# Windowed attention in a hybrid RWKV-7 layer: 128-query blocks with TensorE turns, or 32-query groups over 160 keys with VectorE turns

## The chip, the cores and the metric

The kernel runs on one core of one Trainium2 chip. The metric is the device time of one execution in microseconds (us); lower is better. A profile of one execution gives the start and length of each instruction on TensorE (PE for its matmuls, PEld for its weight loads), VectorE (DVE), ScalarE (ACT) and the transfers that SyncE (SP) issues.

## What is computed

One layer over 2048 tokens of width 1024: an RMS norm, one input projection of 2560 columns, an RWKV-7 recurrence of 8 heads beside windowed attention of 8 query heads on 2 key heads (64 wide each), an output projection, an MLP of width 4096, a gated embedding and a last norm. Of the attention, this is what the change touches:

```python
qi = jnp.arange(BLOCK)[:, None] + BLOCK        # BLOCK = WINDOW = 128
ki = jnp.arange(2 * BLOCK)[None, :]
dist = qi - ki
valid = (dist >= 0) & (dist < WINDOW) & (blk * BLOCK + ki[None] - BLOCK >= 0)
logits = jnp.einsum('bnqhgd,bnkhd->bnhgqk', qb, kw) * ATTN_SCALE + bias
logits = jnp.where(valid[None, :, None, None], logits, -jnp.inf)
m = jnp.maximum(jnp.max(logits, axis=-1, keepdims=True), sink)
e = jnp.exp(logits - m)
probs = e / (jnp.sum(e, axis=-1, keepdims=True) + jnp.exp(sink - m))
out = jnp.einsum('bnhgqk,bnkhd->bnqhgd', probs, vw)
```

A query sees the 128 keys up to itself. A block of 128 queries therefore needs 256 keys; a group of 32 queries needs 160 (its own 32 and the 128 ahead of them, rounded to blocks of 32).

## The kernel before

**Two streams in one.** The 2048 tokens are 16 tiles of 128. The projection (`proj`, four blocks of 512 tokens) and everything behind the mixing (`fin`, four blocks) are long rows of large matmuls of 512 columns, each product computed three times from a split into a high and a low part. One weight chunk is 24 such matmuls; ACT makes its high part (line 991), DVE its low part (line 1312). The mixing of a tile (`mix`, recurrence and attention) is many small operations with long chains between engines. `side_by_side` interleaves them by hand: every engine's program yields after each half chunk of the large work ("a piece", 12 large matmuls) and after each of 27 steps of a tile, and the lists BESIDE_PROJ and BESIDE_FIN say after how many pieces of the large work each step of a tile comes. BESIDE_PROJ places tiles 0 to 3 beside the rest of the projection; BESIDE_FIN places four tiles beside each of the first three `fin` blocks (called here the first to fourth tile of a block). Two steps with the same number have no large matmuls between them. All engines follow the same list, each in its strict order; `Marks` are counting semaphores with one name for each finished operation. The last `fin` block has no tiles beside it.

**The steps around attention, on TensorE.** Step 9: `av` (697), `keys` (the tile's values turned by one 128x128 transpose, 702), `att0` (scores of two of four query-head pairs, line 605: 64-row tiles, 256 keys). Steps 10 to 14: `mz0` to `mz4` (713), five levels of a triangular inverse, 32 matmuls in 32x32 tiles each, in the four diagonal places of the array. With `mz2` goes `turn0` (614, eight 128x128 transposes of probabilities), with `mz3` go `pv0` (622, probabilities by values) and `att1` (605). Step 15: `q` (728). Step 16: `b` (735) and `turn1`. Step 17: `pv1`, `uw` (748 and 754). Steps 18 to 21: `sa0` (762), `grow0` (770, 771), `sa1`, `grow1`, then `y_in` and `y`.

**On VectorE.** Each level is three dependent operations: z (1507), up (1510) and m (1514, a transpose in 32x32 blocks); `mz` of level l waits for m of level l. `logits(n)` (1388 to 1403) comes in steps 9 and 13, `probabilities(n)` (1407 to 1411) in steps 11 and 15, the copy `wT` (1552) between `uw` and `sa0`, the copy `sa` (1415) between `sa0` and `grow0`. The DVE's share of the large work (w_lo 1312; 1634 and 1637 in the first MLP matmul; 1622 where the norm is applied) stands between the steps.

**On ScalarE.** exps (1078, 1080), the copies of the turned probabilities (`pt`), of the result (`att`) and of the values (`vk`), all at line 1084.

Of the kernel before, what the change touches and what calls it, by code (L numbers as in the profile page):

```python
# [9 lines left out]
ALU = mybir.AluOpType  # L10
# [24 lines left out]
LEVELS = 5  # L35

# [68 lines left out]
class Marks:  # L105
# [12 lines left out]
    def done(self, n, step):  # L118
# [14 lines left out]
MIX_PE = (["lora", "gate", "norm", "spread", "bonus", "beta", "alpha", "kappa"] + upto("score", 4) + ["av", "keys", "att0", "mz0", "mz1",  # L133
           "mz2", "turn0", "mz3", "pv0", "att1", "mz4", "q", "b", "turn1", "pv1", "uw",
           "sa0", "grow0", "sa1", "grow1", "y_in", "y", "out"])
MIX_ACT = ["tanh", "sig_g", "kk_sq", "sw", "av", "nrm", "kk_wide", "p_inc", "p_inv", "p_exc", "gate", "beta_t", "avt", "vk",
           "exp0", "esink0", "pt0", "att0", "exp1", "esink1", "pt1", "att1", "y_rms"]
# [3 lines left out]
MIX_DVE = (["kk_raw", "cum", "ascale", "kk_max", "kk_inv", "cumx", "kmod", "v_t", "kk", "kka", "alpha", "beta", "rk", "kappa", "ends", "rho", "yb", "alpha_t", "kappa_t"]  # L141
           + upto("mask", 4) + ["init", "up0", "m0"] + logits_of(0) + level_of(1) + level_of(2) + probs_of(0) + level_of(3)
           + level_of(4) + logits_of(1) + [f"z{LEVELS}", "inv_t", "inv", "xt64", "q"] + probs_of(1)
           + ["b", "wT", "sa0", "grow0", "state0", "sa1", "grow1", "state1", "y_sum", "y_mean", "y", "y_sq", "y_var", "y_inv", "y_norm", "rw", "rw_yb", "rw_gate"])
MIX_STEPS = 27
# [16 lines left out]
for _turned, _last in (("turn0", "out1_3"), ("xt0", "ple1_3")):  # L162
# [18 lines left out]
BESIDE_PROJ = (3, 5, 5, 5, 6, 7, 9, 11, 13, 14, 15, 17, 19, 20, 22, 24, 26, 27, 27, 28, 29, 29, 29, 29, 29, 31, 31, 31, 34, 34, 34, 35,  # L181
# [3 lines left out]
BESIDE_FIN = (0, 1, 2, 4, 4, 4, 6, 6, 10, 12, 13, 16, 18, 22, 23, 25, 28, 29, 31, 32, 33, 34, 34, 35, 38, 38, 40, 40, 40, 44, 46, 46,  # L185
# [3 lines left out]


# [1589 lines left out]
```

## Time and profile before

| | |
|---|---|
| median of 3 runs | 2844.11 us (2841.38 to 2848.77) |
| profiled execution, span | 2842.6 us |
| TensorE matmuls busy | 2784.0 us, 98% |
| VectorE busy | 1737.4 us, 61% |
| ScalarE busy | 1167.5 us, 41% |
| mean DMA rate | 112 GB/s |

How to read it: matmuls overlap, and each is recorded for as long as it takes to come out of the array, so the cost of a group of them is the distance from its first start to the start of what follows, not the sum of their lengths. A float32 matmul that isn't a transpose leaves two records (a count of x8 is four matmuls). Merged rows of the timeline give start, length, engine, line, operands and count, and in square brackets how long the engine sat idle before it and who released it.

### The profile page before, as it was taken

Reading aid. Unit: us, or ns where it says so; the run is one execution under the profiler, and the core shown is the slowest. Engines: PE = TensorE matmul, PEld = TensorE weight load, DVE = VectorE, ACT = ScalarE, POOL = GpSimd, SP = SyncE. Lnnn points to the kernel's source line nnn. Section 1 sums busy time; section 2 is a strip of 40 time slices with the busy share of each in tenths; the row PEclk is TensorE's granted clock in tenths of the full one; section 3 lists DMA queues with packets and bytes.
Section 4 is the critical chain, followed back from the end, with each engine's and each line's share of the span. In section 5 each row is a group of like instructions: output and inputs, shape, how many; then the busy total and the mean of one; then the engine's idle time right before and its main releaser. Section 6 shows DMA issues by size and latency. Waiting matters only on the chain.

```text
span 2842.6 us, 54416 instructions
## 1 busy us (share of the span) xinstructions
PE 2784.0 (98%) x23651; PEld 2251.3 (79%) x23651; DVE 1737.4 (61%) x2886; ACT 1167.5 (41%) x1942; POOL 0.2 (0%) x4
## 2 busy tenths in 40 slices
PE   8999999999999999999999999999999999999998
PEld 6877777777878787878887777878887788888876
DVE  5476676756666565675756566766575655443335
ACT  4354344344433342564333334543343335332225
POOL 0000000000000000000000000000000000000000
PEclk9999999999999999999999999999999999999999
DMA  6553443453333232343332333423333225233332
GB/s 211 162 167 97 146 130 97 136 178 98 89 95 95 86 96 93 122 157 91 92 93 85 96 96 130 155 75 92 101 95 87 84 96 185 89 96 97 97 101 77
DMA packets 369738, 317.47 MB, mean 112 GB/s; under 512 B 47291, under 2 KB 322012, under 8 KB 369500
## 3 DMA queue, kind: packets, MB, share of 16 engines
q1 hardware_dynamic: 365104, 309.58, 35.7%
q10 hardware_dynamic: 4396, 4.41, 0.5%
q8 instruction: 187, 3.06, 0.4%
q14 instruction: 51, 0.42, 0.0%
HBM read 276.18 MB, written 39.32 MB: 111 GB/s over the span
## 4 chain that ended last, share of the span: by engine, by line
PE 78%; DVE 2%; DMA 1%; ACT 1%; issue 0%; SPq 0%; ACTq 0%
PE ps L829 13%; PE ps L833 12%; PE ps L832 12%; PE ps L871 9%; PE ps L875 8%; PE ps L874 8%; PE ps L713 1%; PE ps L583 1%; PE ps L586 1%; PE ps L587 1%; PE ps L605 1%; DMA wraw_f<-in_w_gate 1%; PE ps L614 1%; PE ps L622 1%; PE ps L685 1%; PE ps L628 1%
## 5 line engine op out<-in xcount | busy, mean ns | idle before, releaser
L1312 DVE TENSOR_TENSOR w_lo<-wraw_f,w_hi 128x1024 fp32r<-128x1024 f32 x408 | 498.8, 1222 | 405.4 <-ACT w_hi L991 404.5
L991 ACT ACTIVATE w_hi<-wraw_f 128x1024 fp32r<-128x1024 f32 x408 | 430.9, 1056 | 553.4 <-PE ps L829 462.8
L829 PE MATMUL ps<-w_hi,h_hi 128*128 128x512 f32 x1280 | 513.0, 401 | 7.2 <-DVE rw L1583 4.4
L833 PE MATMUL ps<-w_hi,h_lo 128*128 128x512 f32 x1280 | 499.6, 390 | 0.0
L832 PE MATMUL ps<-w_lo,h_hi 128*128 128x512 f32 x1280 | 498.8, 390 | 0.0
L871 PE MATMUL ps<-act_hi,w_hi 128*128 128x512 f32 x1024 | 408.4, 399 | 0.4
L875 PE MATMUL ps<-act_hi,w_lo 128*128 128x512 f32 x1024 | 399.3, 390 | 0.0
L874 PE MATMUL ps<-act_lo,w_hi 128*128 128x512 f32 x1024 | 398.9, 390 | 0.0
L829 PEld LDWEIGHTS ps<-w_hi,h_hi 128*128 128x128 f32 x1280 | 240.3, 188 | 62.8 <-issue 7.9
L833 PEld LDWEIGHTS ps<-w_hi,h_lo 128*128 128x128 f32 x1280 | 240.2, 188 | 52.3
L832 PEld LDWEIGHTS ps<-w_lo,h_hi 128*128 128x128 f32 x1280 | 240.7, 188 | 46.4
L1192 ACT ACTIVATE h_hi<-tmp 128x512 fp32r<-128x512 f32 x128 | 80.9, 632 | 405.7 <-DVE tmp L1634 405.7
L871 PEld LDWEIGHTS ps<-act_hi,w_hi 128*128 128x128 f32 x1024 | 192.2, 188 | 43.5 <-issue 3.7
L875 PEld LDWEIGHTS ps<-act_hi,w_lo 128*128 128x128 f32 x1024 | 192.2, 188 | 41.2
L874 PEld LDWEIGHTS ps<-act_lo,w_hi 128*128 128x128 f32 x1024 | 192.4, 188 | 37.5
L1637 DVE TENSOR_TENSOR h_lo<-tmp,h_hi 128x512 fp32r<-128x512 f32 x128 | 88.7, 693 | 159.5 <-ACT tmp L1193 159.5
L1634 DVE SCALAR_TENSOR_TENSOR tmp<-ps,stage_f 128x512 f32<-128x512 f32 x128 | 88.2, 689 | 117.5 <-PE ps L875 114.8
L583 PE MATMUL ps<-act_hi,w_hi 128*128 128x512 f32 x320 | 129.9, 406 | 5.5 <-DVE rw L1583 2.9
L583 PE MATMUL ps<-h_hi,w_hi 128*128 128x512 f32 x320 | 129.2, 404 | 2.8 <-DVE rw L1583 1.5
L829 PE MATMUL ps<-w_hi,act_hi 128*128 128x512 f32 x320 | 127.4, 398 | 2.7 <-DVE w_lo L1312 2.3
L587 PE MATMUL ps<-act_hi,w_lo 128*128 128x512 f32 x320 | 125.8, 393 | 0.0
L586 PE MATMUL ps<-act_lo,w_hi 128*128 128x512 f32 x320 | 125.8, 393 | 0.0
(231 smaller groups left out, 4078.8 us busy)
## 6 DMA issues: line engine op xcount, KB each, us to landing
wraw_f<-in_w_ff_up SPq DMA_DIRECT2D x256, 256.0 KB, 3.3
wraw_f<-in_w_ff_down SPq DMA_DIRECT2D x128, 512.0 KB, 4.0
wraw_f<-in_w_in SPq DMA_DIRECT2D x80, 512.0 KB, 4.3
zT<-tmp SPq DMA_DIRECT2D x80, 256.0 KB, 2.1
wraw_f<-in_w_out SPq DMA_DIRECT2D x32, 512.0 KB, 4.0
wraw_f<-in_w_gate SPq DMA_DIRECT2D x32, 512.0 KB, 5.1
zs<-zT SPq DMA_DIRECT2D x16, 896.0 KB, 6.6
h_lo<-mixT SPq DMA_DIRECT2D x4, 2048.0 KB, 8.1
```

The lines of the kernel that those rows point to most:

```text
L583: mm = T.matmul(dst, wh, hi[:, k, :], start=(k == 0), stop=False)
L586: T.matmul(dst, wh, lo[:, k, :], start=False, stop=False)
L587: mm = T.matmul(dst, wl, hi[:, k, :], start=False, stop=(k == DK - 1))
L829: mm = T.matmul(ps[:, j, :], ah, wh, start=(first and k == 0), stop=False)
L832: T.matmul(ps[:, j, :], ah, wl, start=False, stop=False)
L833: mm = T.matmul(ps[:, j, :], al, wh, start=False, stop=(final and k == 1))
L871: mm = T.matmul(ps[:, bank, :], wh, act_hi[:, k, :], start=(k == 0), stop=False)
L874: T.matmul(ps[:, bank, :], wh, act_lo[:, k, :], start=False, stop=False)
L875: mm = T.matmul(ps[:, bank, :], wl, act_hi[:, k, :], start=False, stop=(k == DK - 1))
L991: S.activation(w_hi[:, n % 2, :], raw[:, n % 4, :], ACT.Copy).then_inc(w_hi_done, 1)
L1312: V.tensor_tensor(w_lo[:, n % 2, :], raw[:, n % 4, :], w_hi[:, n % 2, :].bitcast(F32), ALU.subtract).then_inc(w_lo_done, 1)
L1637: V.tensor_tensor(h_lo[:, i, :], tmp[:, i % 2, :], h_hi[:, i, :].bitcast(F32), ALU.subtract).then_inc(fin_dve.mark(f"h_lo{g}_{i}"), 1)
```

## The change

- Scores: for each of four query-head pairs, each group of 32 queries is multiplied with its own 160 keys, for both key heads: 16 matmuls for each round, in tiles of 64 rows by 32 columns of the array, 160 columns moved. Before: 4 matmuls for each round, 64x128, 256 columns.
- The bias, the logits, the exps and the normalisation go over 160 instead of 256 keys.
- The probabilities are turned in 32x32 blocks by VectorE (`pt0`, `pt1`, two transposes of 128x640) instead of 16 TensorE transposes and two ACT copies. Values come by four transfers for each tile into `v_raw`, staggered by 32 keys for each 32 partitions, and one VectorE transpose of 128x640 (`v_turn`, step 10) makes `v_win`, in place of the TensorE turn and the ACT copy `vk`.
- Probabilities by values is one step of its own for both rounds (`pv`, step 17 of now 28): 40 matmuls in tiles of 32 rows by 64 columns, 128 columns moved, into four banks. It waits for `b` and `pt1`. One ACT copy (`att`) in place of two.
- `att1` moves from `mz3` to `mz1`; `logits(1)` moves from VectorE's step 13 (behind m4) to step 12 (behind m3, ahead of z4). `uw` and what follows moves one step down. The lists of places get 28 numbers for each tile.

```diff
-MIX_PE = ([...] + ["av", "keys", "att0", "mz0", "mz1",
-           "mz2", "turn0", "mz3", "pv0", "att1", "mz4", "q", "b", "turn1", "pv1", "uw",
+MIX_PE = ([...] + ["av", "att0", "mz0", "mz1", "att1",
+           "mz2", "mz3", "mz4", "q", "b", "pv", "uw",
-probs_of = lambda n: [f"{s}{n}" for s in ("den", "inv", "probs")]
+probs_of = lambda n: [f"{s}{n}" for s in ("den", "inv", "probs", "pt")]
...
                     def scores(r):
                         for j in (2 * r, 2 * r + 1):
-                            for kv in range(2):
-                                rows = half64(kv)
-                                mm = T.matmul(ps[:, M1 + kv, (j % 2) * 2 * P:(j % 2 + 1) * 2 * P], qT[rows, j, :], kvT[rows, 0, :],
-                                              start=True, stop=True)
+                            for i in range(P // SUB):
+                                for kv in range(2):
+                                    rows = half64(kv)
+                                    mm = T.matmul(ps[sub32(i), M1 + kv, (j % 2) * KEYS:(j % 2 + 1) * KEYS], qT[rows, j, sub32(i)],
+                                                  kT[rows, i * SUB:i * SUB + KEYS], start=True, stop=True)
...
+                    def probs_by_values():
+                        for m in range(SEEN):
+                            for i in range(P // SUB):
+                                for kv in range(2):
+                                    mm = T.matmul(ps[half64(kv), M0 + i, 0:P], v_win[sub32(i), m, half64(kv)],
+                                                  pt[sub32(i), kv, :, m * SUB:(m + 1) * SUB], start=(m == 0), stop=(m == SEEN - 1))
+                        mm.then_inc(mix_pe.mark("pv"), 1)
...
-                        if l == 2:
-                            turn_probs(0)
-                        if l == 3:
-                            probs_by_values(0)
+                        if l == 1:
+                            after(mix_dve, "logit0")
                             scores(1)
...
                     mm.then_inc(mix_pe.mark("b"), 1)
-                    turn_probs(1)
-                    yield
-
-                    after(mix_act, "att0")
-                    probs_by_values(1)
+                    yield
+
+                    after(mix_dve, "b")
+                    after(mix_dve, "pt1")
+                    probs_by_values()
+                    yield
+
                     after(mix_dve, "xt64")
-                    after(mix_dve, "b")
+                    after(mix_act, "att")
... (SyncE)
-                    sp.dma_start(kvT[:, :, at:], zT[RWT + PAIRS:ZT, :, t * P + at:(t + 2) * P].rearrange(
-                        "f p t -> p f t")).then_inc(qkv_in, 16)
+                    sp.dma_start(kT[:, at:], zT[RWT + PAIRS, :, t * P + at:(t + 2) * P]).then_inc(qkv_in, 16)
+                    if t:
+                        sp.wait_ge(*mix_dve.done(t - 1, "v_turn"))
+                    for i in range(P // SUB):
+                        m0 = 0 if t else P // SUB - i
+                        cols = slice(t * P + (i + m0) * SUB, t * P + (i + SEEN) * SUB)
+                        sp.dma_start(v_raw[sub32(i), :, m0 * SUB:], zT[ZT - 1, :, cols].rearrange("(b d) t -> d b t", d=SUB)).then_inc(qkv_in, 16)
... (VectorE)
+                        own(f"probs{n}")
+                        V.transpose(pt[:, :, 2 * n:2 * n + 2, :]..., logit...).then_inc(mix_dve.mark(f"pt{n}"), 1)
...
+                        if step == 10:
+                            dve.wait_ge(qkv_in, 16 * (2 + P // SUB) * (t + 1))
+                            V.transpose(v_win[...], v_raw[...]).then_inc(mix_dve.mark("v_turn"), 1)
                         if step == 11:
                             probabilities(0)
-                        if step == 13:
+                        if step == 12:
+                            own("pt0")
                             logits(1)
```

Of the new places these pairs have no large matmuls between them: `mz3` and `mz4` in the second and third tile of a block (59, 59 and 97, 97, as before); `uw` and `sa0` in the same tiles (66, 66 and 104, 104; before 65, 66 and 103, 104), since `pv` has `uw`'s old place; in tile 0 `uw`, `sa0`, `grow0` (28), in tile 1 all from `uw` to `y` (56), in tile 2 `uw` to `y` (85), in tile 3 `uw` and `sa0` (113). In tile 2 `mz2` and `mz3` have none either (79, as before).

## Rows read from the trace of the kernel before

**Rows 1.** The page: busy time by engine, and the chain that ended last.
```profile
PE 2784.0 (98%) x23651; PEld 2251.3 (79%) x23651; DVE 1737.4 (61%) x2886; ACT 1167.5 (41%) x1942; POOL 0.2 (0%) x4
...
PE 78%; DVE 2%; DMA 1%; ACT 1%; issue 0%; SPq 0%; ACTq 0%
```
**Rows 2.** Timeline of TensorE (start, length, line, operands): attention's operations in two tiles.
```profile
912.78 0.33 PE L702 MATMUL ps<-con,kvT 128*128 128x128 f32 x1
913.04 1.14 PE L605 MATMUL ps<-kvT,qT 64*128 64x256 f32 x8
914.10 0.50 PE L871 MATMUL ps<-act_hi,w_hi 128*128 128x512 f32 x1
...
1096.69 1.08 PE L622 MATMUL ps<-work,vk 128*64 128x256 f32 x8
1097.70 1.13 PE L605 MATMUL ps<-kvT,qT 64*128 64x256 f32 x8
...
1117.74 1.09 PE L614 MATMUL ps<-con,work 128*128 128x128 f32 x8
1118.59 0.47 PE L829 MATMUL ps<-w_hi,h_hi 128*128 128x512 f32 x1
```
**Rows 3.** Timeline of TensorE: groups in small tiles of the array.
```profile
1001.31 0.69 PE L802 MATMUL ps<-state,pp 64*64 64x64 f32 x32
...
1061.89 1.98 PE L685 MATMUL ps<-pp,work 64*64 64x128 f32 x64
...
1087.91 0.75 PE L713 MATMUL ps<-work,small 32*32 32x32 f32 x64
...
1091.55 0.75 PE L713 MATMUL ps<-work,small 32*32 32x32 f32 x64
```
**Rows 4.** VectorE's transpose of 128x512, by form (count, busy, mean ns).
```profile
L1456 DVE STREAM_TRANSPOSE v_t<-kappa_t 128x512 f32<-128x512 f32 x16 | 11.3, 705 | 0.0
```
**Rows 5.** SyncE's own waits: weight loads (us in total, times, longest).
```profile
SPq L374 <- DVE w_lo L1312: 1125.5, 236, 11.7
```
**Rows 6.** Timeline, TensorE and VectorE, levels 3 and 4 of a block's second tile.
```profile
818.20 0.45 DVE L1514 STREAM_TRANSPOSE small<-work 128x256 f32<-128x256 f32 x1
818.56 1.20 DVE L1312 TENSOR_TENSOR w_lo<-wraw_f,w_hi 128x1024 fp32r<-128x1024 f32 x1
819.11 0.75 PE L713 MATMUL ps<-work,small 32*32 32x32 f32 x64
...
821.88 0.75 PE L713 MATMUL ps<-work,small 32*32 32x32 f32 x64
821.99 1.29 DVE L1388 SCALAR_TENSOR_TENSOR work<-ps,bias 128x512 f32<-128x512 f32 x2 [0.72 <-PE ps L605]
...
824.92 0.42 DVE L1523 TENSOR_TENSOR work<-ps,work 128x256 f32<-128x256 f32 x1
```
**Rows 7.** The same levels in the block's third tile.
```profile
953.25 0.75 PE L713 MATMUL ps<-work,small 32*32 32x32 f32 x64
...
955.56 0.45 DVE L1514 STREAM_TRANSPOSE small<-work 128x256 f32<-128x256 f32 x1
956.06 0.75 PE L713 MATMUL ps<-work,small 32*32 32x32 f32 x64
```
**Rows 8.** Timeline, first tile of a block, where the MLP's norm is applied.
```profile
678.33 1.09 PE L614 MATMUL ps<-con,work 128*128 128x128 f32 x8 [0.76 <-DVE work L1411]
...
682.15 1.40 DVE L1622 SCALAR_TENSOR_TENSOR act_lo<-ps,par,act_hi 128x512 fp32r<-128x512 f32 x2
```
**Rows 9.** Timeline of TensorE, tile 2: `uw` with `sa0` right behind it.
```profile
450.45 1.15 PE L754 MATMUL ps<-work 64*64 64x64 f32 x32
...
452.39 0.68 PE L762 MATMUL ps<-state,work 64*64 64x64 f32 x16 [0.79 <-DVE work L1552]
```
**Rows 10.** A long wait of TensorE, and the window behind it (the column ahead of the last two: granted clock).
```profile
252.78 0.80 PE L583 MATMUL ps<-act_hi,w_hi 128*128 128x512 f32 x1 [2.90 <-DVE rw L1583]
...
252.00:256.00 4.00, 3.22 (x8) 2.57 (x9) 2.71 (x6) 0.96 (x3) 0.00 (x0) 0.50 0.66 192
```

More of the change, by code:

```diff
@@ L35 @@
 LEVELS = 5
+SEEN = P // SUB + 1
+KEYS = SEEN * SUB
 PV = {}
@@ L448, in mix @@
                             load_rw(t + 1)
-                        if step == 18:
-                            sp.wait_ge(*mix_act.done(t, "att1"))
+                        if step == 19:
+                            sp.wait_ge(*mix_act.done(t, "att"))
                             sp.dma_start(mixT[PAIRS:, :, t * P:(t + 1) * P].rearrange("f p t -> p f t"), attT).then_inc(att_stored, 16)
-                        if step == 22 and t < TILES - 1:
+                        if step == 23 and t < TILES - 1:
                             sp.wait_ge(*mix_pe.done(t, "grow1"))
                             load_v(t + 1)
-                        if step == 26:
+                        if step == 27:
                             sp.wait_ge(*mix_dve.done(t, "rw_gate"))
@@ L618, in probs_by_values @@
-                    def probs_by_values(r):
-                        after(mix_act, f"pt{r}")
-                        for b in range(2):
-                            for kv in range(2):
-                                mm = T.matmul(pv_ps[half64(kv), :], vk[:, (t + 1 + b) % 2, kv * HD:(kv + 1) * HD],
-                                              pt[:, kv, b, :, :], start=(b == 0), stop=(b == 1))
-                        mm.then_inc(mix_pe.mark(f"pv{r}"), 1)
+                            for i in range(P // SUB):
[3 more added lines that the diff above has]
+                                                  kT[rows, i * SUB:i * SUB + KEYS], start=True, stop=True)
@@ L699, in mix @@
                     mm.then_inc(mix_pe.mark("av"), 1)
-                    pe.wait_ge(qkv_in, 32 * (t + 1))
-                    for b in range(1 if t else 0, 2):
-                        mm = T.transpose(pv_ps[:, b * P:(b + 1) * P], kvT[:, 1, b * P:(b + 1) * P], ident)
-                    mm.then_inc(mix_pe.mark("keys"), 1)
+                    pe.wait_ge(qkv_in, 16 * (2 + P // SUB) * (t + 1))
                     scores(0)
@@ L749, in mix @@
                                      xt64[tok64(c), quad(f, a), :], start=True, stop=True)
-                    after(mix_act, "att1")
                     for h in range(HEADS):
@@ L1391, in logits @@
                             o.then_inc(set_up, 1)
-                            dve.wait_ge(set_up, 7 + n)
-                            o = V.tensor_scalar(logit[:, :, 0:P], logit[:, :, 0:P], NEG, None, ALU.add)
+                            dve.wait_ge(set_up, 8 + n)
+                            for i in range(P // SUB):
+                                before = logit[sub32(i), :, 0:P - i * SUB]
+                                o = V.tensor_scalar(before, before, NEG, None, ALU.add)
                         o.then_inc(mix_dve.mark(f"logit{n}"), 1)
@@ L1516, in mix @@
                             logits(0)
+                        if step == 10:
+                            dve.wait_ge(qkv_in, 16 * (2 + P // SUB) * (t + 1))
+                            if t:
+                                dve.wait_ge(*mix_pe.done(t - 1, "pv"))
+                            V.transpose(v_win[:, :, :].rearrange("p m (b d) -> p m b d", d=SUB), v_raw[:, :, :].rearrange("p b (m t) -> p m b t", t=SUB)).then_inc(
+                                mix_dve.mark("v_turn"), 1)
                         if step == 11:
                             probabilities(0)
-                        if step == 13:
+                        if step == 12:
+                            own("pt0")
                             logits(1)
```

96 lines of the change are left out of this document (41 added, 55 removed), and 13 rows, old and new, of tables (BESIDE_FIN, BESIDE_PROJ).

## The prediction

> **What bounds the kernel now.** I read the page's busy times first, then the chain that ended last, then the timeline around each attention step, engine by engine. TensorE is busy 98% of the span, and the chain runs over TensorE for 78% and over VectorE for 2% [rows 1]: the large matmuls stand almost end to end, and whatever is put between them is paid in full unless something hides in a wait that is there anyway. VectorE has 39% of the span free, but it works in the fixed order of the steps, so what counts there is not its sum but when a result that TensorE waits for is late. Two things have to be worked out: TensorE time removed, and new waits.
>
> **TensorE time, for each tile.** Costs are distances between starts [rows 2].
> - Removed: the turn of the values and round 0's scores, 912.78 to 914.10: 1.32 us. Round 1's scores, 913.04 to 914.10 for the same four matmuls: 1.06. Values, 1096.69 to 1097.70: 1.01, twice. Turns, 1117.74 to 1118.59: 0.85, twice. Together 1.32 + 1.06 + 2.02 + 1.70 = 6.10 us.
> - Added, in smaller tiles. From two groups in 64x64 tiles [rows 3]: 64 records of 128 columns took 1.98 us and 32 of 64 columns 0.69, so 6144 more columns cost 1.29: 0.21 ns a column with four tiles at work, and 0.26 us fixed. In 32x32 tiles 64 records of 32 columns took 0.75, so a record needs no more than (0.75 - 0.26)/64 = 7.7 ns beyond the fixed part. The new scores fall on 2 x 4 = 8 tiles in turn and so do the values (4 x 2). No row shows eight at once. If they overlap as the four do, a column costs 0.105 ns: scores 32 records x 160 x 0.105 = 0.54 a round, values 80 x 128 x 0.105 = 1.07. If only four overlap: 1.07 and 2.15. I take eight with a tenth on top, since two column tiles of one row half already overlapped in the 64x64 group: 0.6 a round and 1.2. A change of tile shape: `pv0` is 8 records of 256 columns with two tiles at once, at 0.42 ns a column 0.86, and it took 1.01, so 0.15 [rows 2]. The `pv` step stands alone between large matmuls: at least the fixed 0.26; I take 0.4, with the restart of the large ones. New: 2 x 0.75 + 1.6 = 3.1 us.
> - Gain 6.1 - 3.1 = 3.0, between 2.9 + 0.3 = 3.2 (eight tiles, nothing on top) and 3.0 - 1.9 = 1.1 (four tiles). Sixteen tiles: 48 us, with ends 51 and 18.
>
> A rule that speaks against the small tiles: the Trainium skill (TensorEngine Tiling (Array Packing), Instruction Overhead) says that each matmul carries about 60 cycles of overhead and that a short one takes as long as one of 60 columns. At its 25 ns a record the new 144 records for each tile would cost 3.6 us instead of 2.4, some 19 us more over sixteen tiles. The trace does not agree for diagonal tiles: the 64 records in 0.75 us are at most 11.7 ns apart [rows 3].
>
> **VectorE, ScalarE and the transfers.** `logits` took 821.99 to 824.92 = 2.93 us [rows 6]; over 5/8 of the columns it is between 1.8 and 2.93, and with small operations and starts unchanged I take 2.15. The normalisation shrinks likewise by about 0.4, each new transpose of 128x640 costs 0.705 x 640/512 less its fixed part, so 0.84 [rows 4]. For each tile: minus 2 x 0.78, minus 2 x 0.4, plus 3 x 0.84 = about zero. In sum nothing, but the order shifts: each `probabilities` is 0.45 longer, and `logits(1)` stands ahead of z4. ScalarE loses the copies of `pt` and `vk`, about 3 us a tile, at 41% busy: worth nothing itself. SyncE issues four more transfers a tile, ahead of weight loads in its queue; it waited 1125 us for w_lo before weight loads [rows 5], so they hide, and cost at most a late weight load where that slack is used up. Its new wait for `v_turn` is for step 10, long done at step 14.
>
> **New waits, place by place.** A piece of large matmuls lasts about 2.9 us (3.64 between two `mz` starts less 0.75 [rows 3]).
> - *Second tile of a block, levels 3 and 4 (three times).* Before, m3 ended at 818.65, `mz3` started at 819.11, then `pv0` and `att1` covered z4, up4, m4 and `mz4` started at 821.88 [rows 6]. Now `mz3` could start 0.85 earlier but waits for m3: 0.4 lost. VectorE then does `logits(1)` (2.15) and w_lo (1.2), and only then z4, up4, m4 (about 1.35): `mz4` at 818.65 + 4.7 = 823.35, where TensorE is free at 819.4. Wait 3.9 + 0.4 = 4.3; three times: 13 us.
> - *Third tile (three times).* `logits(1)` is done long before, but m4 ended only at 956.01 and `mz4` started at 956.06, 2.81 after `mz3` [rows 7]. That is VectorE's time, not `pv0`'s and `att1`'s; without them TensorE waits 2.1 of it: 6.3 us.
> - *First tile (three times).* `turn0` waited 0.76 here, which goes; but at 682.15 VectorE makes act_lo for the first MLP matmul [rows 8], which TensorE follows closely, and now `logits(1)` and 0.45 of `pt0` stand ahead. The chain from there over ACT's square root to the first MLP results moves by about 2 us where TensorE's sum says zero: 6.3 us. One piece later `mz4` finds m4 late by about 1.1, the cover of `pv0` and `att1` gone: 3.3 us.
> - *`uw` and `sa0` without a piece between.* From `uw`'s last group to `sa0` took 1.94, of it 0.79 idle and some 0.15 more in a half-filled array, while `wT` was copied [rows 9]: 0.95 lost. New in the third tile (three times: 2.9). In the second VectorE is in L1634 and L1637 with ScalarE's squares between when `uw` ends: 1.85, three times 5.6. Tiles 0 to 3 get one more such pair each, 0.95: 3.8. Together 12.3.
> - *Smaller.* Tile 1, levels 3 and 4, 1.3; tile 2, levels 2 and 3, 0.85 (the wait for m3 is there already); `mz0` of the second tile 0.3 each; `pv` waiting for `b` behind the longer `probabilities(1)`, 0.8 in all: 3.9.
>
> Sum 13 + 6.3 + 9.6 + 12.3 + 3.9 = 45 us.
>
> - *The clock.* Behind a wait of 2.90 us the granted clock was 0.50 in the next window [rows 10], which is 1.2 GHz: 2 of its 4 us lost, and I take 3 with what lies on either side. The waits of 3.9 in the second tile are longer. I count one such drop in two: 3 x 0.5 x 3 = 4 us (bounds 0 and 9).
>
> **The sum.** -48 + 45 + 4 = +1 us. Its zero is the profiled execution, whose span of 2842.6 lies 1.5 below the median of 2844.1; I move the median by the same. 2844.1 + 1 = 2845; since ScalarE's lighter load can only bring w_hi earlier, I put 3 off for waits that it shortens: 2842.
>
> **Rivals.**
> 1. *The waits are half of what I work out.* VectorE catches up in each wait, and one delay can pay for the next one that I count (the two in the first tile, `uw` behind `mz4`). For it: the places are counted one by one. Against it: between them stand whole pieces, in which VectorE idles anyway. Then -48 + 25 = -23: 2820.
> 2. *The clock falls behind most new waits: slower.* Place: second tile of the blocks, and tile 1, where `uw` to `y` now come without any large matmul and TensorE alternates between short groups and waits. Price 3 us each; decides if more than half of the about nine places of this kind drop. 9 x 3 = 27 less the 4 counted: 2865. Against: before, most waits near 1.5 us left it at full.
> 3. *Small tiles don't overlap eight deep.* By the price with four: 48 - 18 = 30 us less gain: 2842 + 30 = 2872. The Trainium skill's 60 cycles (same section as above) would give 2842 + 19 = 2861 by the same mechanism.
> 4. *The change doesn't save what it says,* because the removed matmuls stood in waits: that is the third tile, counted above at its 6.3.
>
> **How the numbers follow.** Forecast case (gain and waits cancel, 2842, own range 2830 to 2854): 0.46. Rival 1 (2820, 2808 to 2832): 0.28. Rival 2: 0.14. Rival 3: 0.12. A measurement of this kernel can tell 0.3%, 8.5 us, from no change: 2835.6 to 2852.6. From the forecast case 0.10 faster, 0.30 same, 0.06 slower; from rival 1 0.27 faster, 0.01 same; from 2 and 3 0.24 slower, 0.02 same. Together 0.37, 0.33, 0.30. The range 2815 to 2866 leaves out the lower end of rival 1 and the upper halves of 2 and 3, about 0.2.
>
> **What would show it.** Small tiles: the scores group (16 matmuls) at 0.75 and `pv` at 1.2 to 1.3 from first to last start; at 1.1 and 2.2 rival 3 holds. Waits: `mz4` in the second tile some 4.6 behind `mz3` and held by VectorE's transpose m4; in the third 2.8 as before; `sa0` behind `uw` held by `wT`; TensorE's busy share down from 98% to about 96.5%. Clock: a window below 1.00 behind `mz4` of the second tile. The prediction is wrong if `mz4` of the second tile follows `mz3` at under 3 us (rival 1), or if new waits stand where I see none, above all large matmuls waiting for w_lo.

## The result, and the profile after

| | before | after |
|---|---|---|
| median of 5 runs | 2844.11 us (2841.38 to 2848.77) | 2855.81 us (2851.44 to 2861.4) |
| ratio to before, 95% interval | | 1.0039 [1.0024, 1.0054] |
| profiled execution, span | 2842.6 us | 2851.0 us |

The change makes the kernel slower by 0.4%. Forecast was 2842, no change; 2855.8 lies inside the range (2815 to 2866), in which slower by over 0.3% had a chance of 0.30.

The page of after: busy time by engine, and the chain that ended last. TensorE works 38 us less than in [rows 1] and stands in the chain for 72% where it stood for 78%; VectorE's part went from 2% to 6%, ScalarE's from 1% to 3%.
```profile
PE 2745.8 (96%) x25170; PEld 2227.1 (78%) x25170; DVE 1737.9 (61%) x2941; ACT 1121.2 (39%) x1877; POOL 0.2 (0%) x4
...
PE 72%; DVE 6%; ACT 3%; DMA 1%; issue 1%; SPq 0%; ACTq 0%
```

**The small tiles.** The timeline of TensorE in a block's fourth tile of after, where nothing waits; it answers to [rows 2]. The 32 records of a round's scores take 1094.01 to 1094.71, 0.70 us; the 80 of the values 1123.87 to 1125.23, 1.36 us.
```profile
1094.01 0.77 PE L613 MATMUL ps<-kT,qT 64*32 64x160 f32 x32
1094.71 0.50 PE L824 MATMUL ps<-w_hi,h_hi 128*128 128x512 f32 x1
...
1123.87 1.43 PE L621 MATMUL ps<-work,v_win 32*64 32x128 f32 x80
1125.23 0.50 PE L824 MATMUL ps<-w_hi,h_hi 128*128 128x512 f32 x1
```
Two rounds and the values are 2.8 us a tile, 2.9 with the gap ahead of the values, where 6.1 went: 3.2 us a tile, or 52 us, by this view.

**The waits.** TensorE and VectorE in a block's second tile of after, the place of [rows 6], in order of time. `mz3` waits 0.33, `mz4` 3.74 for VectorE's transpose m4. Between m3 (817.55) and m4 (822.04) VectorE does `logits(1)` (from 817.91) and w_lo (from 820.00). Behind the wait the large matmuls of L866 start 0.41 to 0.43 apart instead of 0.23: the clock is at its lower level.
```profile
817.55 0.45 DVE L1506 STREAM_TRANSPOSE small<-work 128x256 f32<-128x256 f32 x1
817.91 0.85 DVE L1376 SCALAR_TENSOR_TENSOR work<-ps,bias 128x320 f32<-128x320 f32 x2
818.04 0.75 PE L709 MATMUL ps<-work,small 32*32 32x32 f32 x64 [0.33 <-DVE small L1506]
818.80 0.82 DVE L1386 TENSOR_REDUCE top<-work 128x4 f32<-128x640 f32 x1
...
820.00 1.21 DVE L1300 TENSOR_TENSOR w_lo<-wraw_f,w_hi 128x1024 fp32r<-128x1024 f32 x1
821.13 0.41 DVE L1499 TENSOR_TENSOR work<-ps,work 128x256 f32<-128x256 f32 x1
...
822.04 0.45 DVE L1506 STREAM_TRANSPOSE small<-work 128x256 f32<-128x256 f32 x1
822.54 0.75 PE L709 MATMUL ps<-work,small 32*32 32x32 f32 x64 [3.74 <-DVE small L1506]
823.23 0.62 PE L866 MATMUL ps<-act_hi,w_hi 128*128 128x512 f32 x1
823.64 0.63 PE L869 MATMUL ps<-act_lo,w_hi 128*128 128x512 f32 x1
824.07 0.63 PE L870 MATMUL ps<-act_hi,w_lo 128*128 128x512 f32 x1
```
TensorE in the third tile of after, with the VectorE operation that holds it first, the place of [rows 7]: the large matmul L866 waits 0.84 for w_lo, which stood behind `logits(1)`; `mz4` starts 2.80 behind `mz3`, 2.05 of it idle.
```profile
942.07 1.22 DVE L1300 TENSOR_TENSOR w_lo<-wraw_f,w_hi 128x1024 fp32r<-128x1024 f32 x1
943.34 0.50 PE L866 MATMUL ps<-act_hi,w_hi 128*128 128x512 f32 x1 [0.84 <-DVE w_lo L1300]
...
957.17 0.75 PE L709 MATMUL ps<-work,small 32*32 32x32 f32 x64
959.97 1.08 PE L709 MATMUL ps<-work,small 32*32 32x32 f32 x64 [2.05 <-DVE small L1506]
```
The same over the whole span: groups of instructions by line of after (busy, mean ns, then the idle time ahead of them and what ended it): the `mz` steps, `sa0` and `sa1`, and the first line of the MLP's up part.
```profile
L866 PE MATMUL ps<-act_hi,w_hi 128*128 128x512 f32 x1024 | 411.7, 402 | 3.7 <-DVE w_lo L1300 3.3
L709 PE MATMUL ps<-work,small 32*32 32x32 f32 x5120 | 61.1, 195 | 24.4 <-DVE small L1506 24.4
L757 PE MATMUL ps<-state,work 64*64 64x64 f32 x512 | 22.7, 230 | 13.8 <-DVE work L1551 11.8 <-DVE state L1417 2.0
```
And before:
```profile
L871 PE MATMUL ps<-act_hi,w_hi 128*128 128x512 f32 x1024 | 408.4, 399 | 0.4
L713 PE MATMUL ps<-work,small 32*32 32x32 f32 x5120 | 60.2, 194 | 0.4 <-DVE small L1514 0.4
L762 PE MATMUL ps<-state,work 64*64 64x64 f32 x512 | 22.2, 227 | 3.4 <-DVE work L1552 2.4 <-DVE state L1425 1.0
```
So the `mz` steps wait 24.0 us more, `sa` 10.4, L866 3.3.

**The clock.** Windows of the second and third tile of after (busy time of each engine; the column ahead of the last two is the granted clock). Before it is 1.00 in all of them.
```profile
820.00:840.00 20.00, 17.46 (x188) 14.01 (x188) 12.79 (x23) 6.05 (x15) 0.00 (x0) 0.91 0.16 53
960.00:980.00 20.00, 20.00 (x199) 16.18 (x200) 11.55 (x19) 5.26 (x7) 0.00 (x0) 0.91 0.16 51
1400.00:1420.00 20.00, 15.92 (x275) 12.53 (x274) 12.67 (x24) 6.08 (x16) 0.00 (x0) 0.91 0.19 56
```
What is missing to 1.00, times 20 us, summed over all windows of 20 us up to 2840, is 8.8 us before and 24.6 after. The time in which TensorE isn't busy (span less busy time) goes from 58.6 to 105.2 us. The three sums are -52 + 46.6 + 15.8 = +10.4, against +8.4 in the spans.

How sure is the clock's part? Of the 24.6 us, 7.2 lie in windows behind four of the new waits at `mz4` (the three of 3.74 and one of the three of 2.05), where before there is nothing. The other 17.4 lie ahead of 640 us, where before has 6.8 (its last 2.0 are at 2820). That early part isn't firm: the kernels of experiments 3 and 10 below have the same program as after up to there, and their profiles show 10.4 and 13.6. What doesn't hang on one profile is the mean granted clock of all runs: its median is 0.996 before and 0.990 after, and 0.006 of 2850 us is 17 us.

The difference of the starts of `out`, after less before, gives each tile's part:

| us | first | second | third | fourth |
|---|---|---|---|---|
| tiles 0 to 3, together | | | | -3.1 |
| block 1 | +2.0 | +4.6 | +2.2 | -2.8 |
| block 2 | +0.2 | +4.4 | +0.7 | -2.9 |
| block 3 | +0.6 | +4.5 | +0.7 | -2.9 |

The fourth tile, where next to nothing new waits, gains what the prediction gives a tile; the second loses that gain and comes out 4.5 us later besides.

### The profile page after: what moved, and what is told of

The parts are those of the page before. It is cut to its first block, busy times and chain, and to the rows that moved or that the text cites. A ratio compares the mean times of both kernels' runs of the same rounds, so it can differ in the third digit from the quotient of the medians.

```text
span 2851.0 us, 57542 instructions
## 1 busy us (share of the span) xinstructions
PE 2745.8 (96%) x25170; PEld 2227.1 (78%) x25170; DVE 1737.9 (61%) x2941; ACT 1121.2 (39%) x1877; POOL 0.2 (0%) x4
## 4 chain that ended last, share of the span: by engine, by line
PE 72%; DVE 6%; ACT 3%; DMA 1%; issue 1%; SPq 0%; ACTq 0%
PE ps L824 13%; PE ps L828 12%; PE ps L827 12%; PE ps L866 7%; PE ps L870 7%; PE ps L869 7%; PE ps L590 1%; PE ps L593 1%; PE ps L594 1%; PE ps L709 1%; DVE w_lo L1300 1%; DMA wraw_f<-in_w_gate 1%; PE ps L684 1%; DVE tmp L1633 1%; PE ps L621 1%
## 5 line engine op out<-in xcount | busy, mean ns | idle before, releaser
L866 PE MATMUL ps<-act_hi,w_hi 128*128 128x512 f32 x1024 | 411.7, 402 | 3.7 <-DVE w_lo L1300 3.3
L866 PEld LDWEIGHTS ps<-act_hi,w_hi 128*128 128x128 f32 x1024 | 193.5, 189 | 50.5 <-issue 5.0
```

Source lines behind the costliest of these rows:

```text
L866: mm = T.matmul(ps[:, bank, :], wh, act_hi[:, k, :], start=(k == 0), stop=False)
```

## The experiments

My theory: TensorE's gain is real and is eaten by VectorE's order and by pieces that no longer stand in waits, and each wait costs clock besides. All kernels change after, unless said. Ratios are to runs of before that were taken along with each kernel; their medians lie between 2842.8 and 2844.9 us.

**1. The order alone.**
```diff
-           + upto("mask", 4) + ["init", "up0", "m0"] + logits_of(0) + level_of(1) + ["v_turn"] + level_of(2) + probs_of(0) + level_of(3) + logits_of(1)
-           + level_of(4) + [f"z{LEVELS}", "inv_t", "inv", "xt64", "q"] + probs_of(1)
+           + upto("mask", 4) + ["init", "up0", "m0"] + logits_of(0) + level_of(1) + ["v_turn"] + level_of(2) + probs_of(0) + level_of(3)
+           + level_of(4) + logits_of(1) + [f"z{LEVELS}", "inv_t", "inv", "xt64", "q"] + probs_of(1)
...
-                        if step == 12:
+                        if step == 13:
                             own("pt0")
                             logits(1)
-                        if step in (10, 13):
-                            exps(step // 13)
+                        if step in (10, 14):
+                            exps(step // 14)
```


> Only the order of VectorE's and ScalarE's work is changed against the kernel after: round 1's logits stand behind the transpose m4 again, ahead of the reciprocals, and ScalarE's exponentials of round 1 one step later. TensorE's program, all places and all transposes stay. My theory: the place of logits(1) ahead of z4 is what makes TensorE wait in the second tile of a block (mz4 3.75 us behind VectorE's m4 in the profile of after), makes the large matmuls of the third tile wait 0.84 for w_lo, and lengthens the first tile's chain. Expected: mz4 in the second tile held about 1.8 instead of 3.75 (3 x 2 = 6 us), the wait for w_lo in the third tile gone (3 x 0.84 = 2.5), the first tile shorter by up to 2 (3 x 2 = 6 at most, half of it likely), and a granted clock of 1.00 in the window at 820 and its two repeats (about 2 us): together 13 us, so 2843 against 2856 of after, with 2838 to 2848 as bounds. Rival A, the order costs nothing, because VectorE has the same work to do before probabilities(1) and q either way, and the wait moves there: 2856 +- 3, with idle time in front of the values or of the mixing matmuls q instead. Rival B, the loss is in the places (no piece between mz3 and mz4): then mz4 keeps more than 3 us of its wait.

Measured: 2841.51 us, ratio to before 0.9991 [0.9982, 1.0000], 14 less than after. VectorE and TensorE in the second tile: m4 is made before `logits(1)`, and `mz4` waits 1.62.
```profile
819.38 0.45 DVE L1506 STREAM_TRANSPOSE small<-work 128x256 f32<-128x256 f32 x1
819.75 0.85 DVE L1376 SCALAR_TENSOR_TENSOR work<-ps,bias 128x320 f32<-128x320 f32 x2
819.88 0.75 PE L709 MATMUL ps<-work,small 32*32 32x32 f32 x64 [1.62 <-DVE small L1506]
```
The wait for w_lo in the third tile and the second of two waits for act_lo in the first (1.00) are gone, as expected: 3 x (2.1 + 0.8 + 1.0) = 12 us. The window at 820 stays at 0.91, though, and the mean granted clock over all runs stays at 0.990, so the 2 us of clock that were expected did not come. Undoing the order alone wins back the whole loss against before. Both rivals fall, the second as it was worded (more than 3 us of wait at `mz4`); what places are worth is the matter of 5 and 6.

**2. A piece between `uw` and `sa0`,** in the second and in the third tile's places in BESIDE_FIN (piece after which a step comes).
```diff
-second: uw 66, sa0 66, grow0 67    third: uw 104, sa0 104, grow0 105
+second: uw 66, sa0 67, grow0 68    third: uw 104, sa0 105, grow0 106
```


> Only two places are changed against the kernel after: in the second and third tile of a block one piece of large matmuls stands between uw and sa0 again, as in the kernel before. My theory: the two lost covers cost what the profile of after shows, 1.73 us of TensorE waiting for wT three times and 0.79 three times, and the time comes back in full since nothing behind it waits for them: 3 x (1.73 + 0.79) = 7.6 us, so 2848 against 2856. Rival: the wait is only handed on, because the piece now stands ahead of sa0 and sa1, grow and y come as much later: under 2 us, 2854 or more, with sa0's wait gone and idle time at sa1 or y.

Measured: 2852.19 us, 1.0025 [1.0016, 1.0035]: 3.6 less, half of what was expected. The waits did go; `sa0` stands behind a piece without any (lines are 4 lower than in after).
```profile
847.73 1.11 PE L745 MATMUL ps<-work 64*64 64x64 f32 x32
851.72 0.68 PE L753 MATMUL ps<-state,work 64*64 64x64 f32 x16
```
From `uw` to `sa1` the profile shows 1.6 and 0.6 us less in second and third tile, but behind `mz4` the clock fell more often or for longer (window at 820 at 0.84, after 0.91), and the sum over all windows is 29.2 against 24.6. The mean granted clock over all runs, 0.989 against 0.990, points the same way, but one thousandth is as fine as it is known. So that the clock took the rest back is likely and not shown by itself.

**3. The waits filled with large matmuls.**
```diff
                     for l in range(LEVELS):
+                        if l == 4 and t >= TPB and t % TPB in (1, 2):
+                            for _ in range(14 if t % TPB == 1 else 7):
+                                T.matmul(ps[:, M3, :], act_hi[:, 0, 0:P], act_hi[:, 1, :], start=True, stop=True)
```


> Against the kernel after, TensorE gets dummy large matmuls of 512 columns just before mz4: 14 of them (14 x 0.2265 = 3.2 us) in the second tile of each of the three blocks, 7 (1.6 us) in the third. They write a bank that holds nothing at that point, add nothing to the result, and fill most of the waits of 3.75 and 2.05 us with work. Every other engine's program stays. My theory: a wait costs more than its length, because the granted clock falls behind it, and in after that was about 10 to 16 us where the prediction counted 4; a filled wait costs its length alone. Expected: mz4 starts where it did within 0.3 us behind mz3, the windows at 820, 960 and their repeats have a granted clock of 1.00 instead of 0.91, and the time falls by 3 to 6 us: 2851 against 2856, the windows elsewhere unchanged. Rival A, the clock's falls at these places have another cause (they come whatever TensorE does there): 2856 with the same windows below 1.00. Rival B, the dummies come too late or run over the end of the wait: then mz4 starts later, by up to 1 us each, and the time rises by up to 4 us.

Measured: 2848.20 us, 1.0014 [1.0005, 1.0023]: 7.6 less than after, with more work on TensorE. Its timeline in the second tile (lines are 3 higher): `mz4` still starts 4.50 behind `mz3`, and the large matmuls behind it run 0.23 apart.
```profile
816.59 0.75 PE L712 MATMUL ps<-work,small 32*32 32x32 f32 x64 [0.34 <-DVE small L1509]
817.27 3.47 PE L706 MATMUL ps<-act_hi 128*128 128x512 f32 x14
821.09 0.75 PE L712 MATMUL ps<-work,small 32*32 32x32 f32 x64 [0.35 <-DVE small L1509]
821.77 0.50 PE L869 MATMUL ps<-act_hi,w_hi 128*128 128x512 f32 x1
822.11 0.40 PE L872 MATMUL ps<-act_lo,w_hi 128*128 128x512 f32 x1
822.34 0.39 PE L873 MATMUL ps<-act_hi,w_lo 128*128 128x512 f32 x1
```
And the windows of it:
```profile
820.00:840.00 20.00, 19.65 (x204) 15.38 (x202) 13.10 (x24) 6.82 (x13) 0.00 (x0) 1.00 0.17 54
960.00:980.00 20.00, 20.00 (x220) 15.89 (x218) 10.02 (x15) 5.86 (x8) 0.00 (x0) 1.00 0.14 41
1400.00:1420.00 20.00, 19.32 (x235) 15.30 (x234) 14.91 (x29) 6.74 (x16) 0.00 (x0) 1.00 0.18 57
```
The wait for m4 is as long as before, and no window in the three blocks is below 1.00 any more. This is the clock's price by itself: these six waits cost 17 us as waits and some 6 to 8 more through the clock (7.6 between the medians, 7.2 by the windows behind them, 5.7 by the starts of `out` in second and third tiles). It was expected at 3 to 6. The mean granted clock over all runs rises from 0.990 to 0.993.

**4. Without VectorE's new transposes.**
```diff
-V.transpose(pt[:, :, 2 * n:2 * n + 2, :].rearrange("p kv j t -> p kv (j t)"), logit.rearrange("p (kv j) t -> p kv (j t)", kv=2))
+V.transpose(pt[:, 0, 2 * n, 0:SUB], logit[:, 0, 0:SUB])
... (v_turn, in all tiles but the first)
-V.transpose(v_win[...], v_raw[...])
+V.transpose(v_win[:, 0, 0:SUB], v_raw[:, 0, 0:SUB])
```
Each new transpose is cut to one block of 32 columns, so this kernel leaves out most of the attention's probabilities and values.

> Against the kernel after, VectorE's new transposes are cut to one 32-column block: both turns of the probabilities in every tile, and the turn of the values in all tiles but the first of a pass, so the attention's probabilities and values are mostly left out of what is computed. Each then takes about 0.1 us instead of 0.80 to 0.85, some 2.2 us less VectorE work a tile (35 us in sum). Everything else, with the order and the places, stays. My theory: VectorE's sum isn't the matter, only where logits(1) stands; so the second tile's mz4 keeps its 3.75 us wait (no turn stands between mz3 and mz4 there), and only the first tile's chain (0.85 in front of act_lo), the waits for wT in the second and third tile and the values behind probabilities(1) get shorter: 3 to 8 us, 2850 against 2856. Rival: the transposes themselves are the cost, as VectorE is late by them throughout: then about 16 x 1 us or more come back, 2840 or less.

Measured: 2856.14 us, 1.0043 [1.0030, 1.0055], no difference to after. VectorE does those of the probabilities in 212 ns instead of 845, and `mz4` of the second tile waits as before.
```profile
824.39 1.08 PE L709 MATMUL ps<-work,small 32*32 32x32 f32 x64 [3.75 <-DVE small L1506]
...
L1403 DVE STREAM_TRANSPOSE work<-work 128x32 f32<-128x32 f32 x32 | 6.8, 212 | 1.1
```
The rival falls. My 3 to 8 us fell too: each first tile came out 1.2 to 1.5 us shorter in the profile, but the end time shows none of it. The clock is lower here, without an explanation: the mean granted clock over all runs is 0.988 where after has 0.990, some 6 us. So the transposes' own cost, if there is one of a few us, can't be told.

**5 and 6. Order and places together; the places alone.** For 5 the diff is that of 1 with these places, 6 has the places only; in tiles 0 to 3 grow0, sa1, grow1 and y move up to two pieces with `sa0`.
```diff
-second: mz4 59, sa0 66, grow0 67    third: mz4 97, sa0 104, grow0 105
+second: mz4 60, sa0 67, grow0 68    third: mz4 98, sa0 105, grow0 106
-tiles 0 to 3: sa0 28, 56, 85, 113    tile 2: mz1 78, mz2 79
+tiles 0 to 3: sa0 29, 57, 86, 114    tile 2: mz1 77, mz2 78
```


> The order of e1_order (round 1's logits behind m4) and new places together: one piece of large matmuls between mz3 and mz4 and between uw and sa0 in the second and third tile of a block, and in tiles 0 to 3 a piece between uw and sa0, in tile 1 the same for grow0 and sa1, in tile 2 one more between mz2 and mz3. The same work in all, nothing left out. My theory: the change's TensorE gain of about 3.2 us a tile (52 us) is real and was eaten by waits that a place or the order can cover. From e1_order's 2841.5: its waits at mz4 of 1.62 (three times) and 2.05 (three times) lie under a piece of 2.7: 11 us; sa0 behind uw, 1.73 and 0.79 three times each: 7.6; tiles 0 to 3, waits of 0.84, 2.07, 0.79, 0.79 at sa0 and of some 0.8 at the places behind: 5; and with fewer waits less of the granted clock lost, about 5. Together 28: 2814, between 2806 (all in full) and 2824. It is then faster than both kernels, by about 1% than before. Rival A, the waits move on to grow, sa1, y and q, as VectorE and ScalarE set the pace of the mixing's chain: 2830 or more. Rival B, as in e2_uw_sa half of what is saved in waits goes back in clock: about 2825.

> The new places of e5_both alone, with the order of the kernel after (round 1's logits ahead of z4). My theory: order and places overlap at one point alone, mz4 of the second tile, where the wait of 3.75 is longer than the piece of 2.7, so 1 us of it stays three times; beyond that the order's other effects stay lost (0.84 at w_lo in the third tile and about 1 in the first tile's chain, three times each). Against e5_both that is 3 x (1.0 + 0.84 + 1.0) = 9 us and some clock: 2814 + 9 + 2 = 2825, bounds 2818 to 2832. Rival: with the places right the order is worth nothing, VectorE having pieces enough to catch up: within 2 us of e5_both.

Measured: 5 takes 2823.31 us, 0.9932 [0.9919, 0.9946]; 6 takes 2833.39, 0.9961 [0.9948, 0.9973]. Each is faster than before, but by less than expected (2814, 2825); 6 lies outside its bounds. In 5, TensorE in the second tile (lines are 7 lower): `mz4` has no wait left, and a new one of 0.90 stands ahead of `q`. The last rows are of tile 0, where the time was missed: TensorE's `sa1` (L750), then `grow1` (L758), which waits 2.38 for VectorE's copy `sa1` (L1400).
```profile
816.57 0.75 PE L702 MATMUL ps<-work,small 32*32 32x32 f32 x64 [0.34 <-DVE small L1499]
820.24 0.75 PE L702 MATMUL ps<-work,small 32*32 32x32 f32 x64
824.83 0.69 PE L715 MATMUL ps<-work,bm 32*32 32x32 f32 x32 [0.90 <-DVE work L1521]
...
238.91 0.68 PE L750 MATMUL ps<-state,work 64*64 64x64 f32 x16
239.65 0.69 DVE L1342 TENSOR_TENSOR tmp<-line 128x512 f32<-128x512 f32 x1 [2.65 <-ACT line L1044]
...
241.22 0.69 DVE L1400 COPY work<-ps 64x512 f32<-64x512 f32 x1
241.97 0.34 PE L758 MATMUL ps<-v_t,kappa_t 64*64 64x64 f32 x4 [2.38 <-DVE work L1400]
```
The same rows say why. The piece that now stands ahead of `sa1` is the second half of a chunk of the projection. VectorE has to take over that chunk's result, behind ScalarE's copy of it (three operations from L1342 on, 239.65 to 241.2), before it comes to the copy `sa1` in its order. In after the piece ahead of `sa1` is a first half, and `grow1` waits 0.80. The waits of 2.38 in tile 1 and 2.24 in tile 3 have the same three operations ahead of the copy.

Against experiment 1 the three blocks gave 22 us by the profiles (7.4 each, where 6.2 and some clock were expected), tiles 0 to 3 only 1 of 5: there rival A holds, the waits moved on. The profiled run of 1 took 5 us more than its median, though; between the medians of 1 and 5 there are 18 us in all. Rival B names nearly the measured time, but its mechanism doesn't hold: the mean granted clock over all runs rose, from 0.990 in experiment 1 to 0.993. The order is worth 10 us on top of the places, as expected (9 and some clock).

**7. Order, and waits filled:** experiment 1 with the dummies of 3, seven in both tiles.
```diff
-                            for _ in range(14 if t % TPB == 1 else 7):
+                            for _ in range(7):
```


> e1_order with 7 dummy large matmuls (1.6 us) before mz4 in the second and the third tile of each block, which fill the waits of 1.62 and 2.05 us that e1_order has there; places as in after. They add nothing to the result. My theory: the wait's own length stays, its price in granted clock goes: the windows at 820, 960 and their repeats at 1.00, mz4 unmoved, and 3 to 6 us less than e1_order: 2837, bounds 2834 to 2840. Rival: the gain of e3_busy (7.6 us) came from the waits of 3.75 alone, the shorter ones of 1.6 and 2.05 cost no clock: 2841.5 +- 1.5.

Measured: 2835.79 us, 0.9972 [0.9961, 0.9983], 5.7 less than experiment 1. The windows at 820, 960 and 1400 are at 1.00 (experiment 1: 0.91, 0.96, 0.91); the only one below in the three blocks is at 2000, behind a wait of 1.73 at `sa0` that isn't filled. So waits of 1.6 and 2.05 us, taken together, cost clock as well; the rival falls.

**8. Steps behind `sa0` moved on.** As 5, with `y` of tiles 0 to 3, `sa1` of tile 2, `out` of tiles 0 and 2 and the starts of tiles 1 and 3 one or two pieces later, and `mz4` of a block's first tile and `q` of its second one later. In tiles 0, 1 and 3 `sa1` and `grow1` keep their places, so no piece was added at the long waits of 5, though the expectation speaks of one ahead of each step.
```diff
-tile 0: y 30, out 31    tile 1: start 31, y 58    tile 2: sa1 86, y 87, out 88    tile 3: start 88, y 115
+tile 0: y 31, out 32    tile 1: start 33, y 59    tile 2: sa1 87, y 88, out 89    tile 3: start 89, y 116
-first: mz4 23    second: q 61
+first: mz4 24    second: q 62
```


> e5_both with its places mended where its trace still shows waits: in tiles 0 to 3 the steps behind sa0 move along with it, so that a piece stands ahead of each of them and the next tile starts a piece or two later (in e5_both sa1 waited 2.38, 2.38 and 2.25 us and out twice 1.93, since only sa0 had been moved); one more piece ahead of mz4 in a block's first tile (0.97 three times) and ahead of q in its second (0.92 three times). My theory: these are 7 + 4 + 6 = 17 us of waits, of which the moved steps save about half: 2823.3 - 8 = 2815, bounds 2810 to 2820. Rival: in tiles 0 to 3 VectorE and ScalarE set the pace, whatever is moved, and each wait goes to the next step: only the 6 of the blocks come back, less what moves on: 2820 or more.

Measured: 2832.87 us, 0.9966 [0.9953, 0.9978]: 10 more than 5. `grow1` still waits 2.38, 2.38 and 2.25 us, which the edit left alone; up to `out` of the first tile of block 1 the profile lost 11 us, and each first tile behind it 1.7 more. The theory's half of 17 us was wrong. That the chain is late there whatever is moved, as the rival has it, was not tested.

**9. The places in the kernel before.**
```diff
-second: mz4 59    third: mz4 97    tile 2: mz1 78, mz2 79
+second: mz4 60    third: mz4 98    tile 2: mz1 77, mz2 78
```


> The kernel before with the places of e5_both that it lacks: a piece of large matmuls between mz3 and mz4 in the second and third tile of a block, and one piece earlier mz1 and mz2 in tile 2. It has the pieces between uw and sa0 already. This tells whether what e5_both gains is the change's or only that of better places. My theory: in the kernel before pv0 and att1 cover the time in which VectorE makes m4, so these places have nothing to give: 2843 +- 2. Rival: the places would have helped the old form as well: 2838 or less.

Measured: 2847.31 us, 1.0012 [1.0003, 1.0021]: a bit slower, outside my 2 us. What 5 gains is the change's, and not that of places from which the old form would have gained too. Whether other places would speed up the old form was not tried.

**10. The dummies in one small tile.**
```diff
-  T.matmul(ps[:, M3, :], act_hi[:, 0, 0:P], act_hi[:, 1, :], start=True, stop=True)
+  T.matmul(ps[0:SUB, M3, :], act_hi[0:SUB, 0, 0:SUB], act_hi[0:SUB, 1, :], start=True, stop=True)
```


> e3_busy with its dummy matmuls in a single 32x32 tile in place of the whole array: 14 of 512 columns before mz4 in the second tile of a block, 7 in the third. They add nothing to the result. This tells what kind of work keeps the granted clock: TensorE is busy as long as in e3_busy, but with a sixteenth of the array. Theory A, that TensorE has work at all is what counts: as e3_busy, 2848 +- 2, windows at 820 and 960 at 1.00. Theory B, the clock follows how much of the array works: as the kernel after, 2856 +- 2, with those windows near 0.91. I hold A for likelier (0.7), since the mixing's groups in 32x32 tiles stand in windows of full clock throughout. If each dummy takes much longer than the 0.2265 us of a large one, mz4 comes later, by what the trace then shows.

Measured: 2852.82 us, 1.0034 [1.0021, 1.0048], which can't be told from after's 1.0039. Its timeline and its window at 1400: the dummies fill the wait, but the clock is at 0.91 as in after.
```profile
818.54 3.42 PE L706 MATMUL ps<-act_hi 32*32 32x512 f32 x14
822.36 0.75 PE L712 MATMUL ps<-work,small 32*32 32x32 f32 x64 [0.40 <-DVE small L1509]
...
1400.00:1420.00 20.00, 19.26 (x288) 13.91 (x287) 12.66 (x24) 6.06 (x15) 0.00 (x0) 0.91 0.20 61
```
It is 4.6 us more than 3. By the time and by the windows theory B holds against my 0.7 for A: work in one small tile did not keep the clock up where the same time of work in the whole array did.

**11. Order, and places in the blocks alone:** the order of 1, the second and third tile's places of 5, tiles 0 to 3 as in after, and
```diff
-second: q 61
+second: q 62
```


> e5_both with the places of tiles 0 to 3 as in the kernel after: the order of e1_order, and pieces only in the blocks, between mz3 and mz4 and between uw and sa0 in the second and third tile, with q of the second tile one piece later. My theory: in tiles 0 to 3 a moved place saves nothing, since VectorE and ScalarE set the pace there (e5_both against e1_order: 1 us up to the first tile of block 1, and e8_spread, which moved more, lost 7); what e5_both won is won in the blocks. So 2823.3 + 1 - 3 x 0.5 = 2823, bounds 2819 to 2828. Rival: the places of tiles 0 to 3 did matter through the clock: 2829 or more.

Measured: 2819.70 us, 0.9913 [0.9899, 0.9926]: the fastest of all, 24 less than before and 36 less than after. The page, and the `mz` steps with 7.4 us of waiting instead of 24.4:
```profile
PE 2738.0 (97%) x25170; PEld 2219.2 (79%) x25170; DVE 1735.3 (62%) x2941; ACT 1120.6 (40%) x1877; POOL 0.2 (0%) x4
...
L705 PE MATMUL ps<-work,small 32*32 32x32 f32 x5120 | 60.5, 194 | 7.4 <-DVE small L1502 6.3 <-issue 1.0
```
In this profile the clock doesn't fall once in the three blocks. The time is as expected, and the rival falls. By the profiles the 3.6 us between it and 5 are lost in tiles 0 to 3 (3.7 up to the first tile of block 1), where the moved places brought the waits of 2.38; the intervals of the two ratios overlap, so this difference isn't clear of the noise.

**12. Each small matmul twice,** on experiment 11.
```diff
-                        for j in (2 * r, 2 * r + 1):
+                        for j in (2 * r, 2 * r + 1, 2 * r, 2 * r + 1):
-                        for m in range(SEEN):
+                        for m in [*range(SEEN), *range(SEEN)]:
```


> e11_blocks with each small matmul of the change issued twice: the 32 of scores in each round and the 80 of the values, the second time over the first with the same result. This measures the disputed cost of the small tiles end to end, 144 more records a tile. By the prediction's eight tiles at once, 2 x 0.54 + 1.07 = 2.15 us a tile, 34 us in sum: 2823 + 34 = 2857, bounds 2850 to 2862. Rival 3 of the prediction, only four tiles at once: 2 x 1.07 + 2.15 = 4.3 a tile, 69 us: 2892. At the 25 ns a record that the Trainium skill (TensorEngine Tiling (Array Packing), Instruction Overhead) leads to, 144 x 25 ns = 3.6 a tile, 58 us: 2881.

Measured: 2854.83 us, 1.0037 [1.0023, 1.0051], 35.1 more than 11. That is 2.2 us a tile, or 15 ns for each of the 2304 added records. Rival 3 falls end to end: eight tiles do overlap. The Trainium skill (TensorEngine Tiling (Array Packing), Instruction Overhead) gives each matmul an overhead of some 60 cycles; the estimate from it, 25 ns a record, would be 58 us. Measured are 35.1, so it doesn't hold for these tiles.

## Why the prediction was off

**TensorE's gain, 48 predicted: right.** Scores 0.70 (0.75 predicted), values 1.36, or some 1.45 with the gap ahead of them (1.6); 3.2 a tile against 3.0. The fourth tile's -2.8 to -2.9 says the same in time, and experiment 12 confirms the price of the new records.

**The waits, 45 predicted: right in sum, and in place but for one.** Idle time rose by 47. Second tile 4.3 predicted, 0.33 + 3.74 found; third 2.1 and 2.05; first, `mz4`, 1.1 and 0.93 to 0.97, and its waits for act_lo 1.25 and 1.00 where before has 0.76, so 1.5 more for the predicted 2.1; `uw` to `sa0` 12.3, and 10.4 at `sa`. Missed, though named among the signs that would refute it: w_lo behind `logits(1)` in the third tile, 0.84 three times, 2.5 us. That the sum comes out so close is in part luck: what was missed makes up for what was counted too high in the first tile and at `uw` and `sa0`. Rival 1 (half of the waits) falls.

**The clock, 4 predicted: here the forecast broke.** The step was "I count one such drop in two: 3 x 0.5 x 3 = 4 us (bounds 0 and 9)". It counted the second tile alone, and one drop in two. The profile shows a window below 1.00 behind the second tile's wait all three times and, behind the third tile's 2.05, once, and more in tiles 0 to 3: 15.8 us more than before over all windows, and 17 by the mean granted clock of all runs. Experiment 3 gives 6 to 8 us for the six waits alone, experiment 7 nearly 6 us for shorter ones. The sentence "before, most waits near 1.5 us left it at full" was what misled: with the order of experiment 1 a wait of 1.62 was followed by 0.91. So rival 2 comes nearest, at 12 us more than the forecast counted in place of its 23. Whether more than half of its places dropped can't be said, since the early windows differ between executions of the same program.

**The allowance of 3 for ScalarE: nothing.** It had no row behind it. With ScalarE's 46 us less work the large matmuls didn't wait less for their weights: their waits for w_lo sum up to 5.7 us before and 7.8 after.

The sum with the clock put right and the allowance left out is -48 + 45 + 16 = +13; found are +8.4 between the two profiled spans and +11.7 between the medians. **Rival 4** played no part.

The transfers and VectorE's sum were rightly put at nothing: VectorE is busy for 1737.9 us after 1737.4, and experiment 4 takes its new transposes away without effect.

What stays open: why a wait of one and the same length is followed by a fall of the clock in one execution and not in another. Of the six waits at `mz4` in the blocks it fell behind four in after, behind all six in experiments 1 and 2, in 2 for twice as long behind those of 3.75; the sums over the windows are 24.6, 32.4 and 29.2. Each is from a single profile, and that of 1 from a run 5 us above its median.

## What to carry to other kernels

Work that is taken away between two steps of a chain over another engine is cover that is taken away: count the gain only where nothing waits, and give that engine's order a new look, since here one entry in VectorE's order was worth 14 us by itself and seven places another 22, which turned 0.4% slower into 0.9% faster. Price a new wait at its length and at what the clock loses behind it, even at 1.6 us. And before you move a piece of other work into a wait, look at what that piece makes the other engines do: in tiles 0, 1 and 3 it put three operations of VectorE ahead of the copy that TensorE needed next, and a wait of 0.80 became one of 2.38.

## What the runs showed of the hardware

- Eight small tiles of the array (64x32 and 32x64) work side by side: 32 records of 160 columns in 0.70 us, 80 of 128 columns in 1.36. Doubling them cost 35.1 us, 15 ns a record, where the price with eight at once gives 34 and that with four 69.
- Behind waits of TensorE of 1.62 us between small groups the granted clock fell each of the three times (experiment 1, windows at 0.91), and behind those of 3.74 too (after, windows at 0.91, 0.91, and 0.94 with 0.97 next to it). With these waits filled with large matmuls the windows were at 1.00; with the wait of 3.74 filled by matmuls in one 32x32 tile (experiment 10) they were as low as in after.
- VectorE's transpose of 128x640 took 845 ns, of 128x32 212.
